# Two-layer encoder trunk on one core: token-block-first projections, transposed rows by block in PSUM, and new orders of norms and feed-forward

## The reference, cut to what matters

```python
def reference(x, c, ...):
    cond = silu(c)
    for l in range(2):
        sh_a, sc_a, g_a, sh_f, sc_f, g_f = split(cond @ ada_w[l] + ada_b[l], 6)
        h = rms_norm(x, norm_attn[l]) * (1 + sc_a) + sh_a
        y = diff_attention(h, ...) if l == 0 else window_attention(h, ..., k_band, v_band)
        x = x + g_a * y
        h = rms_norm(x, norm_ffn[l]) * (1 + sc_f) + sh_f
        y = swiglu(h, ffn_w_in, ffn_w_out) if l == 0 else moe_swiglu(h, ...)   # 8 experts, top 2
        x = x + g_f * y
        if l == 0:
            k_band, v_band = shared_window_kv(x, cond, kv_ada_w, ...)   # its own norm, shift and scale
    return x
```

## Time and profile before

| | us |
|---|---|
| three executions, timed | 1549.32, 1565.36, 1565.20 |
| their median | 1565.2 |
| span of the profiled execution | 1545.4 |
| of it until the first product of the experts | 556.0 |
| of it the experts | 989.4 |
| TensorE busy | 1475.7 |
| VectorE busy | 1305.6 |
| ScalarE busy | 977.5 |

### The profile page before, as it was taken

The page is one execution under the profiler, slowest core; times in us unless marked ns, Lnnn a source line. Parts: engine busy times, 40 slices in busy tenths (PEclk is TensorE's granted clock), DMA queues, the critical chain, the costliest instruction groups (busy, mean ns, idle before and its releaser), DMA issues.

```text
span 1545.4 us, 22238 instructions
## 1 busy us (share of the span) xinstructions
PE 1475.7 (95%) x6578; PEld 1159.2 (75%) x6578; DVE 1305.6 (84%) x1413; ACT 977.5 (63%) x1247; POOL 88.6 (6%) x127
## 2 busy tenths in 40 slices
PE   5998989999899899999999999999999999999997
PEld 2774777777676678888888888888888888888885
DVE  6797868788787868998898888889889889889896
ACT  2468433334447347776777777776777777776773
POOL 3000121111000001000000000000000000000100
PEclk9999999999999999999999999999999999999999
DMA  9982589899751669999999999999999999999993
GB/s 355 340 331 98 173 295 357 308 342 330 211 162 56 220 202 324 371 364 389 367 357 393 361 357 388 371 361 382 374 363 373 371 370 368 367 368 361 398 394 126
DMA packets 212227, 494.36 MB, mean 320 GB/s; under 512 B 16433, under 2 KB 39185, under 8 KB 212177
## 3 DMA queue, kind: packets, MB, share of 16 engines
q1 hardware_dynamic: 196848, 440.46, 78.7%
q0 software_dynamic: 14528, 51.22, 9.5%
q10 hardware_dynamic: 802, 2.06, 0.4%
HBM read 487.13 MB, written 6.55 MB: 319 GB/s over the span
## 4 chain that ended last, share of the span: by engine, by line
PE 85%; DVE 9%; ACT 2%; issue 2%; DMA 1%; SPq 0%; DVEq 0%; ACTq 0%
PE PS L1593 82%; PE PS L2054 2%; DVE WLO L1017 1%; DMA WRAW<-in_ada_w 1%; DVE MOD L1031 1%; DVE MOD L1052 1%; ACT WHI L660 1%; PE PS L1724 1%; DVE MOD L1041 1%; DVE HT_LO L1094 0%; DVE H L1083 0%; DVE H L1085 0%; DVE X L1165 0%; PE PS L2032 0%; DVE H L1164 0%
## 5 line engine op out<-in xcount | busy, mean ns | idle before, releaser
L1017 DVE TENSOR_TENSOR WLO<-WRAW,WHI 128x1024 fp32r<-128x1024 f32 x790 | 916.0, 1219 | 61.0 <-ACT WHI L660 60.7
L660 ACT ACTIVATE WHI<-WRAW 128x1024 fp32r<-128x1024 f32 x790 | 779.0, 1052 | 79.1 <-PE PS L1593 55.6
L1593 PE MATMUL PS<-WHI,HT_HI 128*128 128x512 f32 x1280 | 516.5, 404 | 19.4 <-DVE WLO L1017 11.5
L1593 PE MATMUL PS<-WLO,HT_HI 128*128 128x512 f32 x1280 | 510.5, 399 | 0.0
L1593 PE MATMUL PS<-WHI,HT_LO 128*128 128x512 f32 x1280 | 436.4, 398 | 0.0
L1593 PEld LDWEIGHTS PS<-WHI,HT_HI 128*128 128x128 f32 x1280 | 242.6, 190 | 78.9 <-issue 19.6
L1593 PEld LDWEIGHTS PS<-WHI,HT_LO 128*128 128x128 f32 x1280 | 242.6, 190 | 59.2
L1593 PEld LDWEIGHTS PS<-WLO,HT_HI 128*128 128x128 f32 x1280 | 242.6, 190 | 55.7 <-issue 0.2
L1593 PE MATMUL PS<-WHI,AT_HI 128*128 128x512 f32 x536 | 216.8, 404 | 2.8 <-DVE AT_LO L1289 1.4
L1593 PE MATMUL PS<-WHI,AT_LO 128*128 128x512 f32 x536 | 211.8, 395 | 0.0
L1593 PE MATMUL PS<-WLO,AT_HI 128*128 128x512 f32 x536 | 211.7, 395 | 0.0
(11 more groups left out here) (209 smaller groups left out, 832.2 us busy)
## 6 DMA issues: line engine op xcount, KB each, us to landing
WRAW<-in_moe_w_in SPq DMA_DIRECT2D x448, 512.0 KB, 6.2
WRAW<-in_moe_w_out SPq DMA_DIRECT2D x224, 512.0 KB, 5.6
WRAW<-in_ada_w SPq DMA_DIRECT2D x48, 512.0 KB, 9.2
SHR<-in_ada_w POOLq DMA_DIRECT2D x48, 512.0 KB, 6.7
WRAW<-in_ffn_w_in SPq DMA_DIRECT2D x88, 256.0 KB, 7.3
WRAW<-in_a_w_qkv SPq DMA_DIRECT2D x24, 512.0 KB, 15.3
WRAW<-in_ffn_w_out SPq DMA_DIRECT2D x22, 512.0 KB, 6.5
SHR<-in_kv_ada_w POOLq DMA_DIRECT2D x16, 512.0 KB, 7.0
```

The lines of the kernel that those rows point to most:

```text
L660: nc.scalar.activation(WHI[:, u.split(k), :], WRAW[:, u.raw(k), :], ACT.Copy).then_inc(w_hi, 1)
L1017: V_.tensor_tensor(WLO[:, u.split(k), :], WRAW[:, u.raw(k), :], f32(WHI[:, u.split(k), :]), ALU.subtract).then_inc(w_lo, 1)
L1593: return nc.tensor.matmul(out, a, b, start=start, stop=stop)
```

## The change

1. **Block first.** `project_by_block` goes through `BLOCK_FIRST`: units 0 to 4 for block 0, units 0 and 1 for block 1, units 5 to 7 for block 0, units 2 to 7 for block 1. The first feed-forward units and the KV units are done for block 0 and then for block 1. Block 1's transposes are hooks inside these (after unit 2 of block 0 in WO and BO), and block 0's next transposes stand after unit 6 of block 1.
2. **Transposed rows by block.** PSUM bank 2i+half now holds four column tiles of one block, and `ht_his` and `ht_los` take a list of (block, half).
3. **Norms.** The mean and the epsilon go into ScalarE's square root (`scale`, `bias`), which takes one op of VectorE away per norm. `scaled` multiplies `x` by the folded scale (one op of 128 x 1024) while the root is made, `norm` then does two ops in place of four. The norm of BQ writes `Q` instead of `H`.
4. **Attention.** `head_norm` is cut in `head_sums` and `head_scale`; the sums of block 0 stand inside attention A (n = 13). Two splits (units 28 and 29) stand on ScalarE inside attention A, one `lo` (unit 12) on VectorE inside attention B, and its `hi` on ScalarE right ahead of attention B.
5. **Feed-forward.** In the six steps with a sum ScalarE does both `hi` and `f_silu` ahead of both halves' copies.
6. **Fillers and hooks.** `keep_clock(0, 4)`, `(6, 16)`, `(4, 20)` and one `(3, 8)` go, the others read `AT_HI`. BQ's `kbt_transposes` move from after unit 1 to after (0, 6). Four of the eight `gate_products` move behind the last `ht_los` ahead of the router.
7. **Experts' start.** The selection matrices lie in `HT_HI`/`HT_LO` as fp32r; `slots` multiplies them with two columns of token numbers in single matmuls, two experts at a time between the units 4 to 7 of the first expert.

```diff
+BLOCK_FIRST = ([(0, k) for k in range(5)] + [(1, 0), (1, 1)] + [(0, k) for k in range(5, KT)]
+               + [(1, k) for k in range(2, KT)])
...
                     c = FF_SUMS.get(it * 2 + b)
                     hi_ff_in(u, range(6 * b, 6 * b + 4), it)
                     f_at(it * 2 + (b + 1))
-                    hi(u, 6 * b + 4)
+                    hi(u, 6 * b + 4, 6 * b + 5)
+                    f_silu(u, 6 * b + 3)
                     if c is not None:
                         mod_half(c, 0)
-                    hi(u, 6 * b + 5)
-                    f_silu(u, 6 * b + 3)
-                    if c is not None:
                         mod_half(c, 1)
...
+            def scaled(i, dst, scale_slot, gains, residuals):
+
                 dve.wait_ge(gain_used, gains)
+                dve.wait_ge(x_new, residuals)
+                V_.tensor_tensor(dst[:, i, :], X[:, i, :], MOD[:, scale_slot, :], ALU.mult).then_inc(h_scaled, 1)
...
-                    chain(V_.scalar_tensor_tensor(H[:, i, cols], X[:, i, cols], nx[:, i, 1:2],
-                                                  MOD[:, scale_slot, cols], ALU.mult, ALU.mult))
-                    V_.tensor_tensor(H[:, i, cols], H[:, i, cols], shift[:, cols], ALU.add
-                                     ).then_inc(h_ready, 1)
+                    V_.scalar_tensor_tensor(dst[:, i, cols], dst[:, i, cols], nx[:, i, 1:2], shift[:, cols],
+                                            ALU.mult, ALU.add).then_inc(h_ready, 1)
...
             load_table(ACT.Exp)
+            hi(u, 12)
             attention("B")
...
+                for i, k in BLOCK_FIRST:
+                    split_ready(u, k)
+                    pe.wait_ge(ht_lo, splits + 2 * i + k // 4 + 1)
+                    last = block_products(u, k, i, bank)
...
-                    for k in range(4 * half, 4 * half + 4):
-                        at = (k % 2) * 256 + i * P
-                        last = nc.tensor.transpose(PS[:, k // 2, at:at + P], src[:, i, k * P:(k + 1) * P], ident)
-                        if i == TB - 1 and k % 2:
-                            last.then_inc(ht_psum, 1)
+                    for k in range(4):
+                        c = half * 512 + k * P
+                        last = nc.tensor.transpose(PS[:, 2 * i + half, k * P:(k + 1) * P], src[:, i, c:c + P], ident)
+                    last.then_inc(ht_psum, 1)
...
             u = Units(U_FF)
-            f_in(u, 0, range(4), True, False, 8)
+            for k in range(FF_IN):
+                f_in_block(u, 0, k)
+                if k == 2:
+                    pe.wait_ge(mod_ready, MOD_READY_EARLY)
+                    ht_transposes(H, h_parts(2, BLOCKS[2:]))
+            for k in range(FF_IN):
+                f_in_block(u, 1, k)
...
-                            last = mm(PS[:, 7, e:e + 1], SEL[:, e, i, :], tokid[:, i:i + 1], i == 0, i == 1)
+                            last = mm(PS[:, 7, 2 * e:2 * e + 2], sel(e, i), tokid[:, i, :],
+                                      i == 0, i == 1)
...
-                e_in(Units(base), range(4, 8))
-                slots()
+                for k in range(4, 8):
+                    slots((2 * k - 8, 2 * k - 7))
+                    e_in(Units(base), (k,))
```

More of the change, by code:

```diff
@@ L815, in block_squares @@
                 nc.scalar.activation(W4[:, 0:width], src, ACT.Square).then_inc(sq_ready, 1)
-                root(ss[:, i, 0:width // 64])
+                root(ss[:, i, 0:width // 64], 64)
             hi(u, *range(2, 14))
@@ L1106, in head_norm, with head_scale @@
+            def head_scale(i, count, heads, width, outputs, done):
                 await_root()
@@ L1110, in head_norm @@
                     V_.tensor_tensor(dst, src, bc(ss[:, i, h0:h1], width), ALU.mult).then_inc(done, 1)
+            def head_norm(i, count, heads, width, squared, outputs, done):
+                head_sums(i, count, heads, squared)
+                head_scale(i, count, heads, width, outputs, done)
             def biased(a, n):
@@ L1158, in attention @@
                         scaled_o(n - 2)
+                    if a == "B" and n == 7:
+                        lo(Units(U_BQ), 12)
+                    if a == "A" and n == 13:
+                        head_sums(0, 5, 8, MOD[:, 0, :])
                 if a == "B":
@@ L1210, in _ @@
             lo(u, 0)
-            ht_los(0)
+            ht_los(0, BY_HALF)
             lo(u, 1)
@@ L1845, in f_in @@
                     s = u.split(k0 + k)
-                    if splits is not None:
-                        pe.wait_ge(ht_lo, splits + max(k, 1) + 1)
                     for kt in range(2):
@@ L1942, in _ @@
-                last.then_inc(w_used, 1)
-            ht_transposes(H, h_parts(4))
+                    last = split_mm(PS[:, 4 + 2 * i, :], HT_HI[:, kk, rows], HT_LO[:, kk, rows], WHI[:, s, cols],
+                                    WLO[:, s, cols], kk == 0, kk == KT - 1)
+                if i:
+                    last.then_inc(w_used, 1)
+                elif k == KT // 2 - 1:
+                    last.then_inc(kv_block, 1)
+            for k in range(KT // 2):
+                kv_block_products(0, k)
@@ new lines, in _ @@
+            pe.wait_ge(mod_ready, MOD_READY_EARLY + 2 * (LATE_SHIFT_F + 1))
+            ht_transposes(H, h_parts(3, BLOCKS[2:]))
+            pe.wait_ge(x_new, 4)
+            pe.wait_ge(ada_used, DVE_FF)
+            for half in range(2):
+                mm(PS[:, 5 + 2 * half, :], ones, MOD[:, LATE_SLOTS[LATE_SCALE_F], half * 512:half * 512 + 512]
+                   ).then_inc(mod_sum, 1)
+            for k in range(KT // 2):
+                kv_block_products(1, k)
+                if k == 2:
+                    ht_transposes(Q, h_parts(4, BLOCKS[:2]))
```

347 lines of the change are left out of this document (193 added, 154 removed).

## The result

The changed kernel takes 1560.05 us, the kernel before 1549.0 us (medians of 20 executions each); the ratio is 1.005, with an interval of 1.0028 to 1.0073. Every ratio here is taken over the executions within 1.5% of the same kernel's fastest and lies near the quotient of their means, not of the medians (here 1.0071), so that one execution of the changed kernel, at 2084.87 us, and the two slowest of e1 stand outside it. The change makes the kernel slower by half a per cent where 0.7% less was forecast. Of the 20 executions of the kernel before, four lie at 1564 to 1566 us and the rest at 1547 to 1551, so the three that the prediction started from had caught the rare level twice. The changed kernel's profiled execution took 1554.6 us; its span is 7.4 us over that of the earlier trace rows.

The account below looks back on a forecast made before the run. TensorE was taken to be full in the experts, so only the first 556 us could gain, at its waits in seams and feed-forward. Terms summed to −10.75 us, from 1565.2 to 1554.4 us, range 1536 to 1572.

Parts of the forecast that it names:

- Attention B: Second attention stage: a `hi` ahead on ScalarE and a `lo` inside on VectorE lengthen it, +1.5 us.
- Rival C: TensorE's clock falls at nine gaps that lose a filler or are new; 1575.5 us, chance 0.14.
- rival D: The changed kernel's median lies at the lower of two levels of execution times; 1538.5 us, chance 0.16.
- WO and the first feed-forward units: WO starts earlier and block 0's 24 products go ahead of the last `ht_los`; −6.5 us.
- The feed-forward steps: Steps with a row sum: `hi` no longer waits for a half sum, steps of 19.15 us; −11.7 us.
- rival B: Memory bounds the feed-forward at 315 GB/s, so its steps stay near 22.9 us; 1566 us, chance 0.16.
- KV: KV stage: four units for block 0, then block 1, wait for `lo` that both blocks covered before; +1 us.
- BQ: BQ stage: waits for unit 4's `lo` and unit 7's `hi`, with half a clock fall; +4.8 us.
- Rival A: The seams stay neutral: BQ's +4.8 and the router's +2.95 go to 0; 1546.7 us, chance 0.16.
- BO and the router: Router's products start earlier, but four gate products delay the logits, with half a clock fall; +2.95 us.
- The slots: Experts' start: single matmuls between units replace 32 passes and the half clock behind them goes; −2 us.

Follow-up runs that it names:

- e1: The changed kernel with the split of unit 12 put back behind attention B on ScalarE and VectorE; 1557.25 us, ratio 0.9999 to the kernel before.
- e2: The kernel before with only ScalarE's `hi` of unit 12 put ahead of attention B; 1565.93 us, ratio 1.009.
- e5: The changed kernel with both TensorE waits at attention B's start filled by filler matmuls (`keep_clock(5, 22)`, seven into bank 4); 1542.88 us, ratio 0.9945.
- e10: The changed kernel with only the second wait of attention B filled, by seven filler matmuls into bank 4; 1543.36 us, ratio 0.9941.
- e6: The kernel before with ScalarE's new feed-forward order and both waits of attention B filled; 1537.81 us, ratio 0.9917.
- e11: The kernel before with only the two waits of attention B filled; 1548.11 us, ratio 0.9978.
- e7: e5 with unit 4's splits ahead of the keys' head norms and unit 7's `hi` ahead of the keys' copies in BQ; 1535.05 us, ratio 0.989.
- e9: e7 with all eight gate products between BO's splits again, none ahead of the router's logits; 1536.53 us, ratio 0.9896.
- e8: e5 with BO's splits of unit 13 and two gate products ahead of block 1's `HT_LO`; 1542.81 us, ratio 0.9953.
- e3: The kernel before with only ScalarE's new order in the feed-forward steps with a row sum; median 1546.41 us, ratio 0.9973.
- e4: The changed kernel with only the first wait of attention B filled, `keep_clock(5, 14)` made `keep_clock(5, 22)`; 1557.57 us, ratio 1.0058.

## Why the prediction was wrong

**The step that failed** is "*Attention B.* … **+1.5**, ends 0 and +2.3". It priced the moved `hi` by its own length, as work that shifts the stage, and looked for the clock elsewhere. The stretch took 15.4 us more (the account's fifth line), because TensorE ran 34 of its 53 us at 1.2 GHz. e2 shows that this one `hi` can cost 17 us, e5 and e10 that filler matmuls give 17 us back. Rival C had the mechanism and the sign, but not the place, since its list left out the two waits inside attention B, which were there before; at the nine places that it did name, the time at the low clock did not grow in sum. It had the size wrong too: it took 1.5 to 2.6 us for a fall, from places where TensorE at once has 512-wide matmuls to run. In attention B the matmuls are mostly 64 to 256 wide and come in small groups, and there the low clock held for some 34 us. The price of a fall is set by how long the clock stays low: by an estimate half of that time, 17 us of the 34 here and 10 of the 20 in e1. Why the clock stays low so long in this stage is open (last section). A chance of 0.14 for a case with nine named places was too little for another reason as well: it had been weighed as if one wait decided, and the rows at 208 us (3 us, no fall) had already shown that waits do not decide alone.

**The starting point.** 1565.2 us was taken as the kernel's time because two of three executions had it. It is the rare level, of about one execution in seven. That the levels lie 16 us apart, and that the span fitted the lower, stood in the prediction; it was the reason for rival D, and should have led on to ask which stage can take 16 us more without a change in the program. The changed kernel's account names it: attention B at half the clock. The 3.9 us between span and fastest execution were misread as well: in the changed kernel and in every later run the span is 1.8 to 1.9 us under the device time of the same execution, so that the 1545.4 us belong to one of some 1547.2, at the lower level.

**Luck.** The measured 1560.05 us lie only 5.7 over the forecast's 1554.4, and inside its range. That is luck: the starting point was 16.2 us too high (1565.2 for 1549.0), which covers the 13.9 that attention B took beyond its term. The shift itself was forecast as −10.75 and came as +7.4 in the spans.

**WO and the first feed-forward units** (−6.5 and −0.8 forecast, −5.3 measured to the first long step). The SiLU came at 201.53, in the range of 200 to 203. But behind the wait for the next weights the 24 matmuls took 7.19 us, where 5.84 is due behind a wait at the full clock, and the granted clock from 196.2 to 211.6 was 0.89. The chain of waits has them:

```profile
204.55 7.19 PE PS L1667 x24
```

The wait was 3.05 us, as before, when the clock held. That is a fall of 1.35 us that the sum had not put there.

**The feed-forward steps**: −11.7 forecast, −10.6 measured, and −10.3 as e6 against e11. The order of ScalarE is the cause, as argued. VectorE still waits, 2.99 us for the `hi` that now stands behind the second half's copy, as the timeline of a changed step shows, but TensorE only the 0.18 us of the forecast. The 0.2 us by which a step is over 19.15 are in the 24 matmuls behind that wait, 5.84 us where the sum has 24 × 0.233 = 5.6. Memory gave 345 GB/s where 359 had been asked, and rival B is refuted.

```profile
252.29 0.60 ACT L879 ACTIVATE Q<-PS 128x512 f32<-128x512 f32 x1 [3.11 <-PE PS L1667]
...
256.80 0.60 ACT L889 ACTIVATE MOD<-PS 128x512 f32<-128x512 f32 x1 [3.05 <-PE PS L1667]
...
258.38 1.22 DVE L1052 TENSOR_TENSOR WLO<-WRAW,WHI 128x1024 fp32r<-128x1024 f32 x1 [2.99 <-ACT WHI L675]
```

**KV** was right (+1.0). **BQ** was right in its places and waits, 2.60 and 3.12 us where 2.7 and 3.25 were worked out, and +5.8 in sum for +4.8. The sum held half a fall of the clock; a whole one came (0.88 from 448 to 456 us). Rival A is refuted. e7 gives 7.8 us back.

**BO and the router**, +3.9 for +2.95: the logits came 43.70 us behind BO's first product (39.62 before), 4.1 later, and the experts' first product 11.0 us behind them, as before. The sum does not follow from its own terms: −1.8 and +4.9 make +3.1, and with half a fall +3.9, which is what was measured, where it has +2.15 and +2.95. The mechanism was put wrong in part. e9 shows, as far as six executions tell, that the four gate products ahead of the logits cost no more than between BO's splits; the waits in BO (1.99 us) and ahead of the router (3.23 us) are there in e8, too.

**The slots**: −2.8 for −2, with the clock at 1.00 from 574 to 578 us, as forecast.

## What to carry to other kernels

A 1 us instruction put ahead of a stage of small matmuls can cost that whole stage half its clock. Before moving work to the seams of such a stage, look there for waits of TensorE (here 1.66 and 1.90 us), and try to fill each by itself with matmuls into a free bank; here seven (1.6 us) in the last of them were enough.

When the executions of one kernel lie at two levels, ask the profile which stage could lose the distance between them at half the clock; and judge a change within a level first, then by how often each level comes. An order change that gains 10 us on the path (e3) showed 3 us in the median until the level was held.

An order by token block needs its splits ready earlier by that order, on every engine: the same lists behind a new order of products cost BQ 7.8 us against repaired ones.

## What the runs showed of the hardware

The clock of TensorE did not fall by the length of a single wait. In the changed kernel and its versions it held through a wait of 1.66 us (e10) and fell at the same place with that wait filled and one of 1.85 us left (e4). In e3, with the same two waits as before, 9 us earlier, seven of twelve executions are at the upper levels and five not. The Trainium skill (TensorE: Matmul & The Clock Gate, "Part 1: The HAM clock gate") says that the low clock is the default and that the window in which activity is looked at runs free of the kernel; levels within one kernel agree with that. By that rule alone the share of falls would be the same for the same waits, and e3 (7 of 12) and the kernel before (4 of 31 beside it) differ, by luck in about 1 of 200 trials; the falls are counted from the times there, not from profiles. What else decides, whether what TensorE did before these waits or where the kernel's start puts them, is open; no run moved attention B alone.

Once low in attention B, the clock stayed so for some 34 us in the changed kernel and in e4, 41 in e2 and 20 in e1, with TensorE hardly ever idle by the records (130 matmuls in 32 us, of 64 to 256 columns and a few of 512). Everywhere else in the first 600 us of the changed kernel and the one before, a low stretch lasted 3 to 7 us. That the width of the matmuls decides is not shown: e1's clock rose in the middle of the stage, among the same matmuls.
